# Work at the seams between blocks: a convolution block's last step by column tiles, and four steps put in another place

## What is computed

```python
def conv_glu_ffn(h, w_in, conv_w, conv_b, w_out):       # conv0, conv1
    a, b = jnp.split(h @ w_in, 2, axis=-1)
    a = depthwise_conv(a, conv_w, width=3, causal) + conv_b
    return (jax.nn.silu(a) * b) @ w_out
x = x + conv_glu_ffn(rmsnorm(x, g), ...)
x = x + 0.5 * _swiglu(_rms(x, g), w_in, w_out)          # glu0 to glu3, without the convolution
k = _rms(h @ w_kv[keys]) * k_gain                       # kv, per head; dilated does so with its queries
```

## Time and profile before

| | |
|---|---|
| runs | 1954.37, 1957.86, 1959.96 us (median 1957.86) |
| profiled execution | 1954.76 us, its span 1952.7 us |
| PE busy | 1894.5 us, 97% of the span, 15516 products |
| DVE, ACT, POOL busy | 61%, 50%, 6% |
| mean granted clock of PE | 0.994 |

### The profile page before, as it was taken

The page is one execution under the profiler, slowest core; times in us unless marked ns, Lnnn a source line. Parts: engine busy times, 40 slices in busy tenths (PEclk is TensorE's granted clock), DMA queues, the critical chain, the costliest instruction groups (busy, mean ns, idle before and its releaser), DMA issues.

```text
span 1952.7 us, 36124 instructions
## 1 busy us (share of the span) xinstructions
PE 1894.5 (97%) x15516; PEld 1811.5 (93%) x15516; DVE 1195.3 (61%) x1387; ACT 976.6 (50%) x1139; POOL 112.6 (6%) x52
## 2 busy tenths in 40 slices
PE   7999999899999989999999999999999998999999
PEld 7879999898999989999999999888999987779999
DVE  7667766655866775558667555533555566647554
ACT  7365444545544454345446343776634456655332
POOL 0000000110000000000000000333000011220000
PEclk9999999999999999999999999999999999999999
DMA  7315454443554445555335554455555546425552
GB/s 272 123 56 187 177 189 155 154 146 104 180 190 168 177 140 204 178 172 176 124 112 194 175 191 172 158 173 174 183 184 181 185 162 178 113 95 194 189 176 104
DMA packets 57977, 320.53 MB, mean 164 GB/s; under 512 B 6144, under 2 KB 19536, under 8 KB 20752
## 3 DMA queue, kind: packets, MB, share of 16 engines
q1 hardware_dynamic: 55968, 314.76, 47.1%
q10 hardware_dynamic: 1904, 4.24, 0.6%
HBM read 317.85 MB, written 1.12 MB: 163 GB/s over the span
## 4 chain that ended last, share of the span: by engine, by line
PE 87%; DVE 7%; ACT 3%; issue 2%; DMA 1%; SPq 0%; DVEq 0%; ACTq 0%
PE bank L396 27%; PE bank L398 26%; PE bank L397 26%; DVE lo L346 2%; ACT hi L340 1%; PE bank L463 1%; PE bank L1905 1%; PE bank L500 1%; PE bank L2256 1%; DVE xl L970 1%; PE bank L481 0%; DMA ring<-in_dq 0%; DVE arena L556 0%; PE bank L1298 0%; DVE x L980 0%
## 5 line engine op out<-in xcount | busy, mean ns | idle before, releaser
L396 PE MATMUL bank<-xh,hi 128*128 128x256 f32 x2960 | 846.9, 286 | 17.5 <-DVE lo L369 9.9
L397 PE MATMUL bank<-xl,hi 128*128 128x256 f32 x2960 | 839.4, 284 | 0.0
L398 PE MATMUL bank<-xh,lo 128*128 128x256 f32 x2960 | 839.2, 283 | 0.0
L346 DVE TENSOR_TENSOR lo<-ring,hi 128x2048 fp32r<-128x2048 f32 x274 | 623.6, 2280 | 304.4 <-ACT hi L340 304.1
L340 ACT ACTIVATE hi<-ring 128x2048 fp32r<-128x2048 f32 x290 | 549.2, 1898 | 418.5 <-PE bank L398 407.4
L396 PEld LDWEIGHTS bank<-xh,hi 128*128 128x128 f32 x2960 | 568.2, 192 | 26.4 <-issue 16.2
L397 PEld LDWEIGHTS bank<-xl,hi 128*128 128x128 f32 x2960 | 568.3, 192 | 2.3 <-issue 1.5
L398 PEld LDWEIGHTS bank<-xh,lo 128*128 128x128 f32 x2960 | 568.2, 192 | 0.5
L396 PE MATMUL bank<-gh,hi 128*128 128x256 f32 x1056 | 300.3, 284 | 9.3 <-DVE gl L900 9.3
L398 PE MATMUL bank<-gh,lo 128*128 128x256 f32 x1056 | 299.3, 283 | 0.0
L397 PE MATMUL bank<-gl,hi 128*128 128x256 f32 x1056 | 299.3, 283 | 0.0
(11 more groups left out here) (256 smaller groups left out, 1863.2 us busy)
## 6 DMA issues: line engine op xcount, KB each, us to landing
ring<-in_ffn_in SPq DMA_DIRECT2D x132, 1024.0 KB, 4.9
ring<-in_ffn_out SPq DMA_DIRECT2D x66, 1024.0 KB, 4.9
ring<-in_kv SPq DMA_DIRECT2D x24, 1024.0 KB, 4.9
ring<-in_hg_in SPq DMA_DIRECT2D x16, 1024.0 KB, 4.8
ring<-in_od_in SPq DMA_DIRECT2D x12, 1024.0 KB, 4.8
ring<-in_dq SPq DMA_DIRECT2D x12, 1024.0 KB, 4.9
ring<-in_ev_in SPq DMA_DIRECT2D x10, 1024.0 KB, 5.1
arena<-rel_rows SPq DMA_DIRECT2D x24, 256.0 KB, 3.6
```

The costliest lines, as they stand in the source:

```text
L346: ns.tensor_tensor(lo[n % RING][:, 0:w], ring[n % RING][:, 0:w], hi[n % RING][:, 0:w].bitcast(F32), ALU.subtract).then_inc(lo_ok[lo_by[n]], 1)
L396: nc.tensor.matmul(out_, lh, rh, start=start, stop=False, **kw)
L397: nc.tensor.matmul(out_, lh, rl, start=False, stop=False, **kw)
L398: return nc.tensor.matmul(out_, ll, rh, start=False, stop=stop, **kw)
```

## The change

- In the last step of conv0 and conv1 (j = 10) DVE and ACT go tile by tile: the first tile's taps, silu, product, high and low part, with the second tile's taps between; the semaphores count one more in each such block. PE's last output does the first tile's part of d = 0 to 3 (12 products), then waits for the second tile and does its part of them (12), then the other 24 as before.
- Behind conv0's last step DVE also makes the low part of fox's second chunk.
- PE does the final norm's statistic between the two column tiles of step 1's first chunk.
- PE does kv's statistic in the middle of chunk 1.
- SP issues dilated's first biases behind chunk 5 instead of chunk 4; DVE scales the gains behind the evacuation of chunks 0 to 3.

```diff
-        def ff_in(pe, j, par, n, F, first, it=None):
...
+                    if between is not None and h == 0 and e == 1:
+                        between(pe)
...
+        def ff_out(pe, j, par, n, F, it=None, tail=False, halves=False):
...
-            for d in range(KT):
+            order = [(d, k) for d in range(KT) for k in range(2)]
+            if halves:
+                order = [(d, 0) for d in range(4)] + [(d, 1) for d in range(4)] + order[8:]
+            for d, k in order:
                 dd = slice(d * P, (d + 1) * P)
-                for k in range(2):
-                    last = product(bank[4 + d // 2][:, (d % 2) * T:(d % 2 + 1) * T], wh[:, k, dd], wl[:, k, dd],
-                                   gh[:, par, k, :], gl[:, par, k, :], False, tail and k == 1, skip_group_check=True)
-                if tail and d in (1, 3, 5):
+                if halves and (d, k) == (0, 1):
+                    pe.wait_ge(ff_act, F + j + 2)
+                last = product(bank[4 + d // 2][:, (d % 2) * T:(d % 2 + 1) * T], wh[:, k, dd], wl[:, k, dd],
+                               gh[:, par, k, :], gl[:, par, k, :], False, tail and k == 1, skip_group_check=True)
+                if k == 1 and tail and d in (1, 3, 5):
                     last.then_inc(y_bank, 1)
...
-            ff_in(pe, 1, 1, n + 2, F, None)
-            if b == FINAL:
-                pe_final_stats(pe)
+            ff_in(pe, 1, 1, n + 2, F, None, None, pe_final_stats if b == FINAL else None)
...
+            A = F + acts_before(b)
...
-            ff_out(pe, NJ - 2, 1, last + 3, F)
-            ff_out(pe, NJ - 1, 0, last + 4, F, None, True)
+            ff_out(pe, NJ - 2, 1, last + 3, A)
+            ff_out(pe, NJ - 1, 0, last + 4, A, None, True, b.startswith("conv"))
...
+        def last_of_conv(dve, j, par, F, A, conv, ub, rs2):
+
+            layer, G = conv
+            C, nt = 3 * (G + j) + 3 * (G // NJ), DFF // P
+
+            def taps(e):
+                for tap in range(3):
+                    w = convv[:, layer, bass.ds(2 * j + (tap * nt + e), 1)]
+                    a, c = ff_a[:, par, e, tap:tap + T], ff_c[:, par, e, :]
+                    if tap == 0:
+                        dve.wait_ge(ff_read, 2 * (F + j) + 3)
+                        nc.vector.tensor_scalar(c, a, w, None, ALU.mult).then_inc(ff_conv, 1)
+                    else:
+                        dve.wait_ge(ff_conv, C + 3 * e + tap)
+                        nc.vector.scalar_tensor_tensor(c, a, w, c, ALU.mult, ALU.add).then_inc(ff_conv, 1)
+
+            def gated(e):
+                dve.wait_ge(ff_silu, A + j + 1 + e)
+                dve.wait_ge(ff_read, 2 * (F + j) + 4)
+                nc.vector.tensor_tensor(ff_g[:, par, e, :], ff_s[:, par, e, :], ff_b[:, par, e, :], ALU.mult).then_inc(ff_prod, 1)
+
+            def low(e):
+                dve.wait_ge(gh_ok, A + j + 1 + e)
+                nc.vector.tensor_tensor(gl[:, par, e, :], ff_g[:, par, e, :], gh[:, par, e, :].bitcast(F32),
+                                        ALU.subtract).then_inc(ff_act, 1)
+
+            taps(0)
+            nc.vector.tensor_tensor(ff_b[:, par, :, :], ub, rs2, ALU.mult).then_inc(ff_read, 1)
+            gated(0)
+            taps(1)
+            low(0)
+            gated(1)
+            low(1)
...
+            if conv is not None and not first and it is None and j == NJ - 1:
+                last_of_conv(dve, j, par, F, A, conv, ub, rs2)
+                lo_until(dve, m + (5 if b == "conv0" else 4))
+                return
...
-                lo_until(dve, m + (5 if par else 4))
+                lo_until(dve, m + (5 if par or b == "conv0" else 4))
...
+            A = F + acts_before(b)
+            if conv is not None and it is None and not first and j == NJ - 1:
+                layer, G = conv
+                for e in range(2):
+                    act.wait_ge(ff_conv, 3 * (G + j) + 3 * (G // NJ) + 3 * (e + 1))
+                    nc.scalar.activation(ff_s[:, par, e, :], ff_c[:, par, e, :], ACT.Silu,
+                                         bias=convv[:, layer, bass.ds(2 * j + (3 * (DFF // P) + e), 1)]).then_inc(ff_silu, 1)
+                    act.wait_ge(ff_prod, A + j + 1 + e)
+                    nc.scalar.activation(gh[:, par, e, :], ff_g[:, par, e, :], ACT.Copy).then_inc(gh_ok, 1)
+                hi_until(act, m + 5)
+                return
...
-                        pe_wide(pe, n0 + c, value_banks(k // 2), k % 2, k % 2 == 0, c == 23, mean if early else None)
+                        pe_wide(pe, n0 + c, value_banks(k // 2), k % 2, k % 2 == 0, c == 23,
+                                mean if early else lambda: pe_stats(pe, "kv"))
...
-                    if c == 0:
-                        pe_stats(pe, "kv")
...
-                for p in {4: [0], 8: [1], 10: [2], 12: [3], 13: [4], 15: [5, 6, 7]}.get(c, []):
+                for p in {5: [0], 8: [1], 10: [2], 12: [3], 13: [4], 15: [5, 6, 7]}.get(c, []):
...
+                for c in range(4):
+                    take_out(dve, c)
                 nc.vector.tensor_scalar(QG[:, :], vecs[:, ROW_QG:ROW_QG + 3], DH ** -0.5, None, ALU.mult).then_inc(qg_ok, 1)
                 dve.wait_ge(qg_ok, 1)
-                for c in range(4):
-                    take_out(dve, c)
                 norms(dve, 0)
```

More of the change, by code:

```diff
@@ L786, in first_xg, with ff_in @@
             return info[b]["prep"]["xg0"]
-        def ff_in(pe, j, par, n, F, first, it=None):
+        def ff_in(pe, j, par, n, F, first, it=None, between=None):
             if first is None:
@@ L804, in ff_in, with acts_before @@
                 last.then_inc(chunk_mul, 1)
-        def ff_out(pe, j, par, n, F, it=None, tail=False):
+        def acts_before(b):
+            return sum(c.startswith("conv") for c in plan[:plan.index(b)])
+        def ff_out(pe, j, par, n, F, it=None, tail=False, halves=False):
             pe.wait_ge(ff_act, F + j + 1)
@@ L839, in pe_ffn @@
                                  skip_group_check=True)
+            A = F + acts_before(b)
             def turn(j0, m0, it):
                 for s in range(2):
-                    ff_out(pe, j0 + s, s, m0 + 3 * s, F, it)
+                    ff_out(pe, j0 + s, s, m0 + 3 * s, A, it)
                     ff_in(pe, j0 + (2 + s), s, m0 + 3 * s + 1, F, None, it)
@@ L848, in pe_ffn @@
             last = n + 4 + CHUNKS_TURN * LOOPED
-            ff_out(pe, NJ - 3, 0, last, F)
+            ff_out(pe, NJ - 3, 0, last, A)
             ff_in(pe, NJ - 1, 0, last + 1, F, None)
-            ff_out(pe, NJ - 2, 1, last + 3, F)
-            ff_out(pe, NJ - 1, 0, last + 4, F, None, True)
+            ff_out(pe, NJ - 2, 1, last + 3, A)
[28 more added lines that the diff above has]
+            low(1)
         def dve_ff_step(dve, b, j, par, F, first, conv, it=None):
@@ L876, in dve_ff_step @@
                 layer, G = conv
-                C = 3 * (G + j)
+                C = 3 * (G + j) + 3 * (G // NJ)
                 nt = DFF // P
@@ L894, in dve_ff_step @@
                 lo_until(dve, m + 4)
-            dve.wait_ge(ff_silu, F + j + 1)
+            dve.wait_ge(ff_silu, A + j + 1)
             dve.wait_ge(ff_read, 2 * (F + j) + 4)
@@ L898, in dve_ff_step @@
                                     ALU.mult).then_inc(ff_prod, 1)
-            dve.wait_ge(gh_ok, F + j + 1)
+            dve.wait_ge(gh_ok, A + j + 1)
             nc.vector.tensor_tensor(gl[:, par, :, :], ff_g[:, par, :, :], gh[:, par, :, :].bitcast(F32),
@@ L924, in act_ff_step @@
                 layer, G = conv
-                act.wait_ge(ff_conv, 3 * (G + j) + 3)
+                act.wait_ge(ff_conv, 3 * (G + j) + 3 * (G // NJ) + 3)
                 for e in range(2):
@@ L929, in act_ff_step @@
                 last.then_inc(ff_silu, 1)
-            act.wait_ge(ff_prod, F + j + 1)
+            act.wait_ge(ff_prod, A + j + 1)
             nc.scalar.activation(gh[:, par, :, :], ff_g[:, par, :, :], ACT.Copy).then_inc(gh_ok, 1)
```

## The result

The changed kernel takes 1941.85 us (median of 5, 1939.78 to 1946.67), the kernel before 1956.73 beside it (5 runs, 1952.78 to 1959.96). The ratio is 0.9928 with a 95% interval of 0.9907 to 0.9949: 14.9 us faster by the medians. The profiled execution has a span of 1937.7 us, 15.0 less. I had said 1936 (1929 to 1945), from a sum of -20.4.

What follows compares the result with a forecast made beforehand. TensorE bounds the kernel (87% of its chain of waits), so only its idle or slow-clock time can be gained. Terms -4.8 + 1.6 - 9.8 - 1.9 - 5.5 give -20.4 us; forecast 1936 us, between 1934.4 and 1937.5, range 1929 to 1945.

Steps and rivals of the forecast that it cites:

- sum of -20.4: Whole kernel: forecast gains and losses at the seams, -4.8 + 1.6 - 9.8 - 1.9 - 5.5 us.
- rival B: Whole kernel: the next late item takes more; fox gives 2, dilated 3.1, kv nothing; 1941 us; chance 0.23.
- Part 1: Last step of conv0 and conv1: working by tiles removes PE's stall before the last output chunk, -1.20 us in each.
- Part 2: conv0 to fox: second chunk's low half before the residual adds, -4.8 us with conv0's tail; PE then pauses 2.5 us.
- The clock drop booked at +1.6: Fox's gate, behind PE's 2.5 us pause: 3.4 us at half speed, costing 1.6 us (bounds 0 and 1.7).
- Part 3: conv1 to glu0: moved final statistic ends the 7.20 us wait, -9.8 us with conv1's 1.2 and slow clock; 0.3 lost.
- Part 4: kv: moved statistic trades the 1.41 us wait for 1.5 us on key squares; -1.9 us, -0.3 with a clock drop.
- Part 5: dilated: later biases and gains' scaling end ScalarE's 5.71 us load wait and PE's wait before scores; -5.5 us (-3.1 to -7).
- two readings of the old time: Whole kernel: 1934.4 us from the profiled execution's 1954.76, 1937.5 as the other reading; median of three old runs 1957.86.

Runs made afterwards that it cites:

- the load early: Changed kernel with ScalarE loading kv's block constants a block earlier, before glu1's steps: 1937.96 us (median of 4), ratio 0.9899 to the kernel before.
- the second profiles: Kernel before and changed kernel, both unaltered, each profiled once more; dilated stretch 58.89 and 54.78 us; changed kernel timed again at 1941.94 us, ratio 0.9923.

## Why the prediction was right or wrong

**The total** lies in the range, but the gain is 5 to 6 us short of the sum of -20.4. It is near rival B's time (1941) by another way than B's: kv gave nothing, as B had it, but fox and dilated, which B had give little, gave their part. The range of 16 us was wide enough to hold a part that went the wrong way. The 20.3 us timed with the load early look like the sum but don't confirm it: their interval reaches from 16.6 to 23.1, and the span of that kernel's profile is 17.1 less than before.

**Part 1**, the tiles: the stall is gone in both blocks. From the start of the evacuation to the end of the low half, the first tile took 4.90 us (5.05 worked out) and the second 6.47 (6.45). Its value was booked as 1.20 in each block. In conv1 some 0.8 of it is seen, 0.72 from PE's overlap. In conv0 PE's overlap is worth nothing behind part 2: with fox's low half in front of the adds, DVE and not PE sets the seam. The rule that small tiles pay a fixed latency each (the Trainium skill, VectorE: DVE Perf Modes, section on the TRN2 errata) agrees with the trace in that half the columns cost 0.42 us and all of them 0.69. It did not decide here, where the tiles let PE begin earlier.

**Part 2**: -5.23 against -4.8. The place of the low half is 4.2 of it. PE's pause at the gate is 1.65 us, not the 2.5 worked out. The clock drop booked at +1.6 is there in one profile of the changed kernel and not in the other, and costs 1.45 when it comes.

**Part 3**: -9.59 against -9.8, with the remaining 0.28 us wait where it was foreseen.

**Part 4** is the step that failed. It said that PE waits 1.5 us for the squares, and gave -1.9. Two terms were wrong. The 1.9 was almost wholly the clock: the sum compared a chunk slowed by a drop that belonged to one execution with one at full speed; at equal clock the edit gives 0.14. And it named the squares as the only thing that the mean waits for. The code has a second wait there, `const_in` for k = 0, and the DMA issue behind ScalarE's root was never costed, although the root was moved to the moment at which SP's next chunk leaves. That is worth 2.1 to 2.3 us in this stretch (16.23 and 16.38 against 14.09), and 0.8 to 1.4 in the next (13.35 and 13.98 against 12.53), since in both profiles half clock follows the wait. Over both stretches kv takes 29.73 and 30.21 us, the kernel before 28.38 with its drop and 26.74 at full clock. How much of that is clock shows in the trace with both tiles' low halves first: kv is not edited in it, PE waits 3.08 us for the load, and there is no drop. It takes 15.98 and 12.51, so at full clock the change loses 28.49 - 26.74 = 1.75 us here, and up to 3.5 with the drop.

**Part 5**: -4.96 against -5.5, one drop of 3.4 us instead of 10.2 behind the scores included; between the second profiles, with 6.8 against 10.2, it is -4.1 (54.78 against 58.89). The mechanism held, but the working treated the two edits as a sum of steps; each has the other as its cover. The trace agrees a second time with the shared port's rule, by which a Vector instruction in a two-port mode and a GpSimd one exclude each other (the Trainium skill, SBUF — State Buffer, section Who interferes with whom): the three-column scaling takes 2.42 us beside POOL's low half and 0.16 without it. That the scaling runs in such a mode is taken from the page; the traces show only its time. What the prediction left open, whether the evacuations are held too, is answered: they take 0.65 us each beside it.

**The level**: I placed 1936 between two readings of the old time. The changed kernel's own runs spread over 6.9 us, nearly half the width of the range. The spans differ by 15.0 us, the sum said 20.4; of the 5.4 us between, kv is 3.2 (-1.9 forecast, +1.35 with the next stretch), the first block's drop 3.5, dilated 0.5, glu0 0.2; fox's absent drop and better seam give 2.0 back.

## What to carry to other kernels

When a step is moved, list every instruction that its successor's queue issues behind it, the DMAs too, and look at what another queue issues at the same moment: a step moved by one microsecond made a 64 KB load leave together with a 1 MB one and land 4 us later. Price a stretch at equal clock before crediting an edit with it, and profile the unaltered kernel twice. Undo edits singly and together, since two of them can hold the same slack.

## What the runs showed of the hardware

The load of kv's constants (64 KB, from ScalarE's queue) landed in 1.8 us when it left 1.1 us ahead of a 1 MB load of SP's, and in 5.8 when both left within 0.01 us. The load behind it (144 KB, in the traces with the constants early) landed in 4.1 us when it left within 0.02 us of such a load, and in 2.7 when it left 1.1 us ahead.

The same kernel with the same 1.41 us pause of PE had the clock at 0.50 behind it in one execution and at 1.00 in another. Behind the pauses of 1.63 to 1.65 us at fox's gate the clock fell in 7 of 11 traces; behind kv's wait for the load (2.9 to 3.7 us) in seven of eight. Drops of 3.4 or 6.8 us came and went in the first block (at 86 to 88, 104 and 140 to 145 us) in kernels that are identical up to there. Between two profiles of one kernel the stretches without them repeat within 0.12 us; over all traces without a drop in it, the first stretch takes 331.18 to 331.55.
